# First projections of a two-branch layer: the tail of each item (norm sum, its roots, its turning) one turn later on TensorE, ScalarE and VectorE

## The reference, cut to what matters

```python
h = rmsnorm(x, norm_mix_g[l])
proj = h @ w_in[l]                       # 1024 -> N_IN
(qa, ka, va, qd, kd, vd, beta_logit, decay_logit, z, gate_logit) = jnp.split(proj, offsets, axis=-1)
...
y_attn = grid_attention(qa, ka, va) @ w_o_attn[l]
qkv = jax.nn.silu(centred_depthwise_conv(jnp.concatenate([qd, kd, vd], axis=-1), dn_conv_w[l]))
qd, kd, vd = jnp.split(qkv, [DN_QK, 2 * DN_QK], axis=-1)     # 8 heads of 64 each
qd = l2norm(qd.reshape(b, s, DN_HEADS, DN_DK)) * (DN_DK ** -0.5)
kd = l2norm(kd.reshape(b, s, DN_HEADS, DN_DK))
...
o = bidir_gated_deltanet(qd, kd, vd, beta, g)                # chunks of 64, both directions
...
x = x + (mixed @ w_out[l])
```

## Time and profile before

| | |
|---|---|
| median of 3 runs | 3276.15 us |
| lowest and highest | 3275.21, 3278.52 us |
| the profiled execution's own time | 3268.41 us |
| its span | 3266.6 us |
| mean granted TensorE clock over the span | 0.997 |
| TensorE busy | 3134.2 us (96%) |
| VectorE, ScalarE, GpSimd busy | 1881.7, 1410.9, 426.6 us |

### The profile page before, as it was taken

One profiled execution on the slowest core, in us unless ns is written; L12 is line 12 of the kernel. 1 busy time (PEld: TensorE's weight loads), 2 busy tenths in 40 slices (PEclk: granted clock), 3 DMA queues, 4 the chain that ended last, 5 costly groups with the idle time before them and its releaser, 6 DMA issues.

```text
span 3266.6 us, 59920 instructions
## 1 busy us (share of the span) xinstructions
PE 3134.2 (96%) x25776; PEld 2480.1 (76%) x25776; DVE 1881.7 (58%) x3058; ACT 1410.9 (43%) x2478; POOL 426.6 (13%) x428
## 2 busy tenths in 40 slices
PE   8899999999999999999999999999999989999999
PEld 5687778888876777878888876767788767676887
DVE  6576657756467676657745665554444655535443
ACT  5645324433246544234423355554433455444432
POOL 0051430000000332500000001121200001203010
PEclk9999999999999999999999999999999999999999
DMA  5001104333332001123333242212132232121223
GB/s 176 28 22 47 41 28 129 100 97 97 97 117 76 21 29 60 36 76 113 97 97 97 87 130 84 88 40 72 58 91 77 89 105 88 46 71 59 83 76 100
DMA packets 80216, 255.03 MB, mean 78 GB/s; under 512 B 11344, under 2 KB 13008, under 8 KB 78928
## 3 DMA queue, kind: packets, MB, share of 16 engines
q1 hardware_dynamic: 79952, 251.19, 24.7%
HBM read 238.08 MB, written 6.29 MB: 75 GB/s over the span
## 4 chain that ended last, share of the span: by engine, by line
PE 77%; DVE 10%; ACT 8%; issue 2%; DMA 2%; POOL 1%; SPq 1%; ACTq 0%; DVEq 0%; POOLq 0%
PE psum L534 74%; PE psum L710 3%; DVE s_wlo L1981 2%; ACT s_tmp L1277 1%; DVE s_xb L1981 1%; ACT s_whi L1277 1%; DVE s_tmp L1984 1%; DMA s_stage<-w 1%; ACT s_E L1277 1%; DVE s_ffy L1984 1%; POOL s_xb L2698 1%; SPq L2832 1%; ACT L1287 1%; DVE psum L1981 0%; ACT L1277 0%
## 5 line engine op out<-in xcount | busy, mean ns | idle before, releaser
L534 PE MATMUL psum<-s_h,s_whi 128*128 128x512 f32 (+1 forms) x4576 | 1453.6, 399 | 14.1 <-DVE s_wlo L1981 6.8
L534 PEld LDWEIGHTS psum<-s_h,s_whi 128*128 128x128 f32 (+1 forms) x4576 | 845.7, 188 | 226.7 <-issue 33.9
L534 PE MATMUL psum<-s_h,s_wlo 128*128 128x512 f32 (+1 forms) x2288 | 895.0, 391 | 0.0
L1981 DVE TENSOR_TENSOR s_wlo<-s_stage,s_whi 128x1024 fp32r<-128x1024 f32 (+2 forms) x468 | 532.5, 1140 | 358.0 <-ACT s_whi L1277 357.2
L1277 ACT ACTIVATE s_whi<-s_stage 128x1024 fp32r<-128x1024 f32 (+2 forms) x468 | 450.0, 966 | 279.9 <-DMA s_stage<-w 80.4
L534 PEld LDWEIGHTS psum<-s_h,s_wlo 128*128 128x128 f32 (+1 forms) x2288 | 430.0, 188 | 94.7
L534 PE MATMUL psum<-s_ffa,s_whi 128*128 128x512 f32 x704 | 217.5, 390 | 4.6 <-DVE s_ffa L1981 4.6
L2698 POOL TENSOR_TENSOR s_xb<-s_xb,s_cstm 64x512 f32<-64x512 f32 x64 | 101.0, 1577 | 897.6 <-DVE s_xb L1981 893.4
L2730 POOL TENSOR_SCALAR s_E<-s_E,s_inv,s_g 128x128 f32<-128x128 f32 (+3 forms) x128 | 77.0, 612 | 1058.2 <-DVE s_inv L2089 1043.5
L1984 DVE SCALAR_TENSOR_TENSOR s_ffy<-psum,s_pcol,s_ffy 128x511 f32<-128x511 f32 x176 | 131.7, 748 | 110.8 <-ACT s_ffy L1277 107.7
L1277 ACT ACTIVATE s_E<-psum,s_nm 128x256 f32<-128x256 f32 (+3 forms) x224 | 114.6, 516 | 174.8 <-DVE s_nm L2067 139.5
(11 more groups left out here) (307 smaller groups left out, 4365.5 us busy)
## 6 DMA issues: line engine op xcount, KB each, us to landing
s_stage<-w SPq DMA_DIRECT2D x192, 512.0 KB, 3.7
s_stage<-wup SPq DMA_DIRECT2D x88, 512.0 KB, 3.6
s_stage<-wo SPq DMA_DIRECT2D x32, 512.0 KB, 3.6
s_stage<-wdn SPq DMA_DIRECT2D x32, 512.0 KB, 3.6
s_stage<-wdn SPq DMA_DIRECT2D x16, 384.0 KB, 3.1
spill<-s_x SPq DMA_DIRECT2D x2, 2048.0 KB, 8.9
s_stage<-woa SPq DMA_DIRECT2D x16, 256.0 KB, 2.6
s_x<-spill SPq DMA_DIRECT2D x2, 2048.0 KB, 7.9
```

The costliest lines, as they stand in the source:

```text
L534: return self.e.matmul(out, left, right, start=first, stop=last, skip_group_check=True)
L1981: return self.e.tensor_tensor(out, a, b, op)
```

## The change

In `project_end` every step that follows the first one is moved back by one turn, on the three engines:

- TensorE: one more `yield` at the start. The sum of a q or k item is issued one turn later, and so is the turning of a k or v item.
- ScalarE: tanh and the square stay where they are; Ln and Exp, and the copies `tok` to s_ktok and s_vtok, come one turn later.
- VectorE: the silu multiply stays; the multiply `out` comes one turn later.

```diff
@@ -876,6 +876,7 @@
 
     def project_end(self, key):
         l, _, g, s3, j = key
+        yield
         if s3 == 2:
             yield
             ps = self.take((key, "T"))
```

## The result

| | before | after |
|---|---|---|
| median of the runs (4 and 4) | 3275.68 us | 3298.13 us |
| lowest and highest | 3272.84, 3278.52 | 3297.46, 3309.24 |
| after against before, with 95% interval | | 1.0077 (1.0064 to 1.0090) |
| the profiled execution's own time | 3268.41 us | 3297.65 us |
| its span | 3266.6 us | 3295.9 us |

The change made the kernel slower, by 0.64 to 0.90%, which is some 25 us. The two profiled executions lie 29.3 us apart; all that follows is read from them, so its parts add up to that figure.

What follows compares the result with a forecast made beforehand. TensorE, busy 96% of the span, was taken as the bound. Phases A +2.9, B +1, C -0.5 made 3.4 us a layer, 6.8 in two, taken as 7.5: 3276.15 - 7.5 = 3268.5 us; forecast 3264 to 3271, range 3261 to 3281.

Runs made afterwards that it cites:

- e6_hold_front: e1 with TensorE's banks of one k item's sum and of the g=1 turnings returned at the head of the free list; 3267.46 us, 0.9989 against before.
- e1: The changed kernel with the fill (attention and products of g=1) not advanced in the first turn of phase B; 3313.10 us, 1.0120 against before.
- e5_g0_hold: The changed kernel with the added yields only for g == 0 and the fill held in phase B's first turn; 3266.30 us, 0.9985 against before.

## What to carry to other kernels

A step moved by a turn makes its phase longer, and what fills the next phase enters it on the other foot: take the stretch behind the edit, where "nothing changes", and lay the two orders side by side before counting anything there. A price read from steps that are covered is no price for them bare. Buffers handed round by a first-in, first-out list are one more queue that a moved step passes: write down for each take whose reader it waits for, before and after.

## What the runs showed of the hardware

- A wait can cost again behind itself. The timeline of TensorE of e6_hold_front has, for the same gate product as e1's at 290.31:

```profile
282.33 0.70 PE L536 MATMUL psum<-s_h,s_whi 128*128 128x512 f32 x2 [0.87 <-ACT s_tmp L1286]
```

  After e1's 5.18 the half product ran in 4.6 us (290.31 to 294.86) and after e6's 0.87 in 3.0 (282.33 to 285.30), its first matmuls at 0.98 us a pair (290.31 to 291.29) against 0.54 (282.33 to 282.87): the granted clock at its lower level (1.2 GHz) for a time after the idle stretch, at the full 2.4 GHz else. In the changed kernel this was 7.4 of the 15.8 us.
- The same order of instructions took from 75.0 to 79.7 us in phase A of l=0 in the kernels with moved tails. The stretch at the lower clock lies in another place; the windows view from 100 to 120 us, after (first row) and e5_g0_hold (second):

```profile
100.00:120.00 20.00, 18.88 (x102) 12.72 (x102) 13.15 (x23) 14.98 (x27) 0.00 (x0) 0.95 0.10 28
100.00:120.00 20.00, 17.53 (x75) 11.38 (x74) 11.08 (x20) 13.22 (x24) 0.00 (x0) 0.83 0.07 26
```

  What sets the place was not found; a single profile can't tell 2 us there.
- VectorE's weight split of 128x1024 took 2.28 and 2.29 us for the two of the 4.50 above, and 1.21 to 1.23 in phase C. The slow ones started while a GpSimd operation of the units was under way; that GpSimd is at work beside a split is not enough. The timelines of VectorE and GpSimd of the kernel before show both cases:

```profile
225.22 3.85 POOL L2698 TENSOR_TENSOR s_xb<-s_xb,s_cstm 64x512 f32<-64x512 f32 x2
225.62 2.31 DVE L1981 TENSOR_TENSOR s_wlo<-s_stage,s_whi 128x1024 fp32r<-128x1024 f32 x1
231.90 1.21 DVE L1981 TENSOR_TENSOR s_wlo<-s_stage,s_whi 128x1024 fp32r<-128x1024 f32 x1
232.06 3.91 POOL L2698 TENSOR_TENSOR s_xb<-s_xb,s_cstm 64x512 f32<-64x512 f32 x2 [1.29 <-DVE s_xb L1981]
```

  At 225.62 the first of the two GpSimd operations had 1.22 us left, and the split took 1.1 us longer; at 247.78 it had 0.94 left and the split took 2.02. At 231.90 the split came first and kept its 1.21. In the traces of all runs, 34 splits during which a GpSimd operation started took 1.21 to 1.23 each. No run changed GpSimd's work to try this.
